# Two-block transformer kernel: where the last two modulation slabs of each layer are multiplied, and on which token tile the layer's output product begins

## The reference, cut to what matters

```python
def ada_params(sc, w, b):          # sc (n, 1024), w (1024, 6144)
    mod = sc @ w + b
    return [t[:, None, :] for t in jnp.split(mod, 6, axis=-1)]

def conv_glu(x, w_in, conv_w, conv_b, w_out):      # first block, both layers
    gate, val = jnp.split(x @ w_in, 2, axis=-1)    # 2 x 2816 columns
    gate = lax.conv_general_dilated(gate, conv_w[:, None, :], ...) + conv_b
    return (jax.nn.gelu(gate, approximate=False) * val) @ w_out

# first block, each layer:
x = layer_norm(ALPHA * x + h, ...)                       # after the mixer
x = layer_norm(ALPHA * x + memory_cross_attention(...), ...)
x = layer_norm(ALPHA * x + conv_glu(x, ...), ...)
# second block: ada_params(silu(c), ada_w[i], ada_b[i]) for its layers i = 0, 1
```

## Time and profile before

| | |
|---|---|
| median of 3 runs | 2130.54 us (2127.76 to 2132.85) |
| the profiled execution, its own time | 2126.64 us |
| its span in the trace | 2124.9 us |
| busy: PE / DVE / ACT / POOL | 1931.2 / 1083.8 / 994.5 / 1258.8 us |
| read from DRAM | 339.65 MB, 160 GB/s over the span |
| mean granted PE clock | 0.963 |

### The profile page before, as it was taken

The page is one execution under the profiler, slowest core; times in us unless marked ns, Lnnn a source line. Parts: engine busy times, 40 slices in busy tenths (PEclk is TensorE's granted clock), DMA queues, the critical chain, the costliest instruction groups (busy, mean ns, idle before and its releaser), DMA issues.

```text
span 2124.9 us, 33890 instructions
## 1 busy us (share of the span) xinstructions
PE 1931.2 (91%) x13581; PEld 1704.6 (80%) x13581; DVE 1083.8 (51%) x1511; ACT 994.5 (47%) x1718; POOL 1258.8 (59%) x588
## 2 busy tenths in 40 slices
PE   6879989999899979989999889998879998978997
PEld 6868888877899966868877868876669987948996
DVE  7783146641100073136657655678767942846641
ACT  3453435443444373434554444478744546425542
POOL 9647566678688602646669334300468885426995
PEclk9999999999899999999999999999989998989999
DMA  6325367764555503357774212211235553314552
GB/s 251 139 93 186 112 224 293 302 259 175 177 181 190 187 1 139 119 220 279 298 274 161 80 62 97 99 60 64 86 135 182 181 194 121 119 61 164 182 192 104
DMA packets 48321, 342.30 MB, mean 161 GB/s; under 512 B 5264, under 2 KB 6288, under 8 KB 7248
## 3 DMA queue, kind: packets, MB, share of 16 engines
q1 hardware_dynamic: 45968, 328.22, 42.3%
q0 software_dynamic: 2240, 12.49, 1.5%
HBM read 339.65 MB, written 1.05 MB: 160 GB/s over the span
## 4 chain that ended last, share of the span: by engine, by line
PE 65%; DVE 17%; ACT 7%; POOL 5%; issue 5%; DMA 1%; DVEq 0%; POOLq 0%; SPq 0%; ACTq 0%
PE bank L1664 11%; PE bank L1668 11%; PE bank L1666 11%; PE bank L1718 11%; DVE arena L902 2%; POOL w_lo L2146 2%; PE bank L1762 2%; PE bank L1277 2%; POOL w_hi L2146 2%; PE bank L1279 2%; PE bank L1280 2%; PE bank L1699 2%; PE bank L1698 2%; PE bank L1696 2%; ACT arena L1102 2%
## 5 line engine op out<-in xcount | busy, mean ns | idle before, releaser
L2146 POOL TENSOR_TENSOR w_lo<-ring,w_hi 128x1024 fp32r<-128x1024 f32 x360 | 876.8, 2461 | 314.4 <-ACT w_hi L2696 313.9
L1664 PE MATMUL bank<-x_hi,w_hi 128*128 128x256 f32 x2176 | 615.7, 283 | 29.9 <-POOL w_lo L2146 16.6
L1668 PE MATMUL bank<-x_lo,w_hi 128*128 128x256 f32 x2176 | 618.4, 284 | 0.0
L2696 ACT ACTIVATE w_hi<-ring 128x1024 fp32r<-128x1024 f32 x448 | 448.7, 1052 | 348.8 <-DMA ring<-slabs_dram 344.7
L1664 PEld LDWEIGHTS bank<-x_hi,w_hi 128*128 128x128 f32 x2176 | 414.4, 190 | 50.5 <-issue 50.5
L1668 PEld LDWEIGHTS bank<-x_lo,w_hi 128*128 128x128 f32 x2176 | 413.6, 190 | 0.0
L1666 PE MATMUL bank<-x_hi,w_lo 128*128 128x256 f32 x1472 | 413.4, 281 | 0.0
L1666 PEld LDWEIGHTS bank<-x_hi,w_lo 128*128 128x128 f32 x1472 | 281.3, 191 | 0.0
L2146 POOL TENSOR_TENSOR w_hi<-ring,w_hi 128x1024 fp32r<-128x1024 f32 x88 | 208.8, 2394 | 110.9 <-ACT w_hi L2696 110.9
L2634 ACT ACTIVATE arena<-bank 128x512 f32<-128x512 f32 (+1 forms) x182 | 100.1, 563 | 296.9 <-PE bank L1668 190.8
L1666 PE MATMUL bank<-x_hi,w_hi 128*128 128x256 f32 x704 | 197.5, 281 | 0.0
(11 more groups left out here) (341 smaller groups left out, 3657.9 us busy)
## 6 DMA issues: line engine op xcount, KB each, us to landing
ring<-slabs_dram SPq DMA_DIRECT2D x312, 1024.0 KB, 4.8
lnrow<-ln_dram POOLq DMA_DIRECT2D x6, 1024.0 KB, 5.0
xt<-xT_dram SPq DMA_DIRECT2D x1, 1024.0 KB, 5.9
xt<-memT_dram POOLq DMA_DIRECT2D x1, 1024.0 KB, 14.0
x<-x_dram POOLq DMA_DIRECT2D x1, 1024.0 KB, 17.9
arena<-ctx_dram POOLq DMA_DIRECT2D x1, 1024.0 KB, 7.0
lnrow<-ln_dram POOLq DMA_DIRECT2D x2, 512.0 KB, 4.8
res<-x POOLq DMA_DIRECT2D x2, 512.0 KB, 3.2
```

What stands on the lines that cost most here:

```text
L1664: ins = pe.matmul(dst, wh[:, k, c], src[0][:, k, :], start=(k == 0), stop=False)
L1668: ins = pe.matmul(dst, wh[:, k, c], src[1][:, k, :], start=False, stop=(k == KC - 1))
L2146: pool.tensor_tensor(dst[:, c], ring[:, s, c], w_hi[:, s, c].bitcast(F32), ALU.subtract).then_inc(S["lo_ready"], 1)
L2696: a.activation(w_hi[:, g % RING, c], ring[:, g % RING, c], ACT.Copy) \
```

## The change

The four modulation slabs 22 and 23 of both layers leave the stream: `f0` and `f1` have 44 slabs, the ring sees 308 loads. The four are loaded into two places of their own in the arena (`aside`), two after output slab 4 of `fo0`, two after slab 2 of `xq1` (the second cross attention's query weights). PE multiplies them in the norm that follows (`late_ada`): the first before the transposes of the first token tile, the second between the two tiles. For layer 0 that is the norm after `fo0`, for layer 1 the norm ahead of network 1. ACT copies them out (`late_out`), DVE turns them (`turn_late`), ACT keeps the columns (`late_columns`). Layer 0's last four chunks are added to the bias with layer 1's.

`rows_split` of `fo0` and `fo1` waits for banks 2 and 3 only, runs slab 0 on the second token tile, waits for banks 0 and 1, and runs slab 0 on the first. ACT makes `hi` of output slab 0 one chunk earlier and of slab 1 where slab 0's was. `ctx` and `wdt` are loaded after POOL's last `lo` of `f1`.

```diff
+ASIDE = {"f0": 2, "f1": 2}
-    STAGES.append((_name, _n))
+    STAGES.append((_name, _n - ASIDE.get(_name, 0)))
...
+        aside = [cut(11264, KC, 256), cut(16384, KC, 256)]
+        late_raw = xT[:, 5:7, :]
+        late_turn = [xT[:, 7, :], xT[:, 0, :]]
...
             def rows_split(stage, src=(h_hi, h_lo), n_slabs=FC // 2, ready=("hT_ready", 2), hook=None):
-                for b_ in (0, 1, 2, 3):
+                second_first = stage in ("fo0", "fo1")
+                for b_ in (2, 3) if second_first else (0, 1, 2, 3):
                     pe.wait_ge(free_of(b_), frees(b_))
...
                     ready_for(j)
+                    if j == 0 and second_first:
+                        tile(j, 1, (0, 1), (0, 1), True)
+                        for b_ in (0, 1):
+                            pe.wait_ge(free_of(b_), frees(b_))
+                        tile(j, 0, (0, 1), (0, 1), False)
+                        continue
...
+            def late_ada(layer, e):
+                b = 6 + e
+                pe.wait_ge(aside_landed[e], 16 * (layer + 1))
+                pe.wait_ge(free_of(b), frees(b))
+                for k in range(KC):
+                    q = 32 * (k % 4)
+                    ins = pe.matmul(bank[b][q:q + 32, 0:256], sc_in[:, k, :], aside[e][:, k, :],
+                                    start=(k < 4), stop=(k >= 4))
+                fill(ins, b, "act")
...
-                    col_T_split(stage, 2 * u + 41, u)
-                ada(stage, 4, 2, 10)
-                ada(stage, 5, 3, 10, last_one=True)
+                    col_T_split(stage, 2 * u + 41, u, last_net=u == 1)
...
-            tokens_to_T(by_class=True)
+            late_ada(0, 0)
+            tokens_to_T(by_class=True, between=lambda: late_ada(0, 1))
...
-            tokens_to_T(used_up=True)
+            late_ada(1, 0)
+            tokens_to_T(used_up=True, between=lambda: late_ada(1, 1))
...
                 if k in (1, 4):
                     los(f"f{k // 4}", 1, 2)
+                    if k == 4:
+                        pool.dma_start(ctxN[:, :, :], ctx_in).then_inc(S["in_ctx"], 16)
+                        pool.dma_start(wdt[:, :, :], wdt_in).then_inc(S["in_wdt"], 16)
...
+                for layer, at in enumerate((FIRST["fo0"] + 4, FIRST["xq1"] + 2)):
+                    if g == at:
+                        for e in range(2):
+                            sp.dma_start(aside[e].rearrange("p a b -> p (a b)"),
+                                         slabs[AT[f"f{layer}"] + 44 + e]) \
+                                .then_inc(aside_landed[e], 16)
...
+            def turn_late(layer):
+                for e in range(2):
+                    v.wait_ge(free["act"][6 + e], marks["late"][layer][6 + e])
+                    v.transpose(late_turn[e], late_raw[:, e, :]).then_inc(S["late_turned"], 1)
+                    v.wait_ge(S["late_turned"], L.own("late_turned"))
...
-                        elif n == FC - 1:
-                            hi(out_, 0)
+                        else:
+                            hi(out_, n + 2 - FC)
```

More of the change, by code:

```diff
@@ L89 @@
     _at += _n
-SLABS = _at
-assert SLABS % RING == 0
+STREAM = _at
+SLABS = sum(_n for _name, _n in DRAM)
+assert STREAM % RING == 0
 RUNS = [("dq", "dwo"), ("xq0", "xk1"), ("gq0", "gwo"), ("xq1", "f1")]
@@ L188, in build @@
         landed = [ctx.enter_context(nc.semaphore(f"slab_landed{s}")) for s in range(RING)]
+        aside_landed = [ctx.enter_context(nc.semaphore(f"aside_landed{s}")) for s in range(2)]
         full = {r: [ctx.enter_context(nc.semaphore(f"full_{r}{b}")) for b in range(8)]
@@ L1886, in ada @@
                                     start=(k < 4), stop=(k >= 4))
-                    begun(ins, k == 0 and last_one)
                 fill(ins, b, "dve")
+            def late_ada(layer, e):
[7 more added lines that the diff above has]
+                fill(ins, b, "act")
+                marks.setdefault("late", {}).setdefault(layer, {})[b] = L.now(("act", b))
             def ada_columns(layer):
                 pe.wait_ge(free_of(4), frees(4))
-                pe.wait_ge(S["ada_kept"], 24 * (layer + 1))
+                pe.wait_ge(S["ada_kept"], 22 * (layer + 1))
+                if layer:
+                    pe.wait_ge(S["late_kept"], 4)
+                n = (22, 24)[layer]
                 kept = modC.rearrange("p u (c q s) -> p q (u c) s", c=2, q=4)
+                late = late_cols.rearrange("p u (c q s) -> p q (u c) s", c=2, q=4)
                 for q in range(4):
-                    ins = pe.matmul(bank[4][32 * q:32 * (q + 1), 0:96].rearrange("p (a s) -> p a s", s=2),
-                                    pick, kept[:, q, :, :], start=True, stop=True)
+                    part = bank[4][32 * q:32 * (q + 1), :].rearrange("p (a s) -> p a s", s=2)
+                    ins = pe.matmul(part[:, 0:2 * n, :], pick, kept[:, q, 0:2 * n, :],
+                                    start=True, stop=True)
+                    if layer:
+                        ins = pe.matmul(part[:, 48:52, :], pick, late[:, q, :, :],
+                                        start=True, stop=True)
                 fill(ins, 4, "dve")
@@ L2230, in _ @@
             for layer in range(2):
-                for n in range(2, FC):
-                    halves_read[FIRST[f"f{layer}"] + 2 * n + 1] = marks[f"lo_f{layer}"] + 2 * (n - 1)
-            for g in range(SLABS):
+                for n in range(FC):
+                    halves_read[FIRST[f"f{layer}"] + 2 * n + 1 + RING] = marks[f"lo_f{layer}"] + 2 * (n + 1)
+            for g in range(STREAM):
                 if g in halves_read:
@@ L2653, in proj_N, with late_out, late_columns, x_to_T @@
                              bank[u][:, :].rearrange("p (t c) -> p t c", t=NT))
-            def x_to_T(by_class=False):
+            def late_out(e):
+                copy_out(6 + e, late_raw[:, e, :], bank[6 + e][:, 0:256])
+            def late_columns(dst):
+                for e in range(2):
+                    a.wait_ge(S["late_turned"], L.took("late_turned"))
+                    a.activation(dst[:, e, :].rearrange("p (c s) -> p c s", s=2),
+                                 late_turn[e].rearrange("p (c s) -> p c s", s=32)[:, :, 0:2],
+                                 ACT.Copy).then_inc(S["late_kept"], 1)
+            def x_to_T(by_class=False, late=False):
                 for tt in range(NT):
@@ L2659, in x_to_T @@
                         b, ck = 4 + 2 * tt + q, slice(4 * q, 4 * q + 4)
+                        if late and q == 0:
+                            late_out(tt)
                         a.wait_ge(full["act"][b], L.filled(b))
@@ L2871, in _ @@
             hi("gq0", 1)
[L2872 removed]
+            x_to_T(by_class=True, late=True)
             a.wait_ge(S["qscale_ready"], DIL_HEADS)
```

54 lines of the change are left out of this document (30 added, 24 removed).

## The result

The changed kernel takes 2113.42 us (median of 5 runs, 2110.81 to 2114.51). The kernel before, beside it, took 2130.54 us (2123.14 to 2132.85). The ratio is 0.9929, with an interval of 0.9917 to 0.9941. The prediction was 2115.4 us, so 15.1 us less; 17.1 came. Run once more with other runs of the kernel before, the changed kernel took 2113.99 us, ratio 0.9922 (0.9909 to 0.9936), 14.6 us less. So the forecast size lies between the two measurements. (In the rounds of the experiments, with 11 to 29 runs each, the median of the kernel before was 2128.2 to 2129.1 us, so 17.1 is on the high side.)

What follows compares the result with a forecast made beforehand. PE, busy 91% of the span, was taken as the bound, so only its standing still or running slowly mattered. 6.95 + 6.98 + 1.6 - 0.4 = 15.1 us off 2130.54 gave 2115.4 us, range 2108 to 2123.

Steps and rivals of the forecast that it cites:

- 1. The ends of both networks: At `fo0` and `fo1`, slab 0 is ready early and slab 1 starts 6.95 and 6.98 us sooner.
- 2. The products in the gaps: In the norms, modulation products moved into PE's gaps before the transposes fit there and cost nothing.
- 3. DVE's turns: Ahead of network 1, DVE's two turns stand before `x_lo` and cost 0.95 us, bounds 0.5 and 1.2.
- 4. Network 1's start: Moving `ctx` and `wdt` removes PE's 2.51 us stall at 958.89; less 0.95 for DVE's turns, net gain 1.6 us.
- the difference, 2.5 us, is the stall: At network 1's start, slab load of 9.8 against 7.3 us beside `ctx`: this 2.5 us was taken as PE's stall.
- The price of `ctx` at its new place: Beside output slabs 2 and 3, the moved load delays them 3.4 us if taken in full; the sum counted nothing.
- 5 and 6: 5: loads aside in `fo0` and `xq1` cost 0, bound 2.4 us each. 6: middle of `fo1` loses 0.4 us.
- Slab 0 was not late: Rival at both network ends: slab 0 is still late, half of part 1 lost, gain 8, 2122.5 us; chance 0.12.
- the stream did not suffer: Rival: loads aside delay a slab at both places and the 958.89 stall stays, gain 7.8, 2122.7 us; chance 0.10.
- the lower clock did not last longer behind the gaps: Rival in both norms: late products as short bursts prolong the low clock; 25 us more in each gives 2140 us; chance 0.03.
- More comes back by the clock: Rival: late products shorten low-clock stretches after 534 and at 940.11, up to 2.5 and 1.7 us; gain 19, 2111.5 us; chance 0.12.

Runs made afterwards that it cites:

- the two experiments on the old stream: Kernel before with one edit each: output slab 0 on the second token tile first, ratio 1.0009; `ctx` and `wdt` loaded after POOL's last subtraction, ratio 1.0008.
- one edit: Kernel before, with only slab 0 of both output products on the second token tile first, waiting for banks 2 and 3 only: 2128.35 us, ratio 1.0009.

## Why the prediction was right

**1. The ends of both networks.** Forecast 6.95 and 6.98, measured 6.8 and 7.0. From the last network matmul to slab 1 of `fo1` it took 13.24 us before (the modulation products, the wait and slab 0) and takes 6.22 now; in `fo0` 13.21 and 6.45. (The table's 7.1 and 6.3 have all of network 0 in them.) Every step of the working is in the profile: ACT takes slab 0 after chunk 20's product and does not wait for the load, POOL is done 0.75 us ahead of PE (0.9 worked out), the wait for banks 0 and 1 is 0.25 to 0.35 (0.1), slab 1 follows at once. Two things make the number: the idle time, and that the clock no longer falls behind it.

**2. The products in the gaps** take no time of PE's path themselves, doubled too. But network 1 starts 1.15 us more slowly in every kernel that has them (below), and the prediction put this part at nothing. That the products are the cause is not shown.

**3. DVE's turns** cost 0.96 us at the wait, as worked out (0.95); 0.5 to 0.7 of it come back when they stand behind `x_lo`.

**4. Network 1's start: the right number for a wrong reason.** Forecast was that the stall of 2.51 us goes, and that `ctx` was its cause. The stall went, and with it the smaller ones behind it, 3.0 us in all. But alone the move took 1.5 us from the stall, lost 0.8 two pairs on and 2.2 at `fo1`; and undone in the changed kernel it costs 0.4 at most. The step that failed is "the difference, 2.5 us, is the stall". The load did become faster, by 1.5 us alone and by 2.0 in the changed kernel, but the step took for granted that all of this stands on PE's path and that the network would start as before. That 1.6 us net came out near what was measured here (3.0 less 1.0 for the turns) is luck. The Trainium skill, DMA: Bandwidth & Descriptors, section Issuing engines are not separate DMA queues, says that transfers started by different engines interleave on the same 16 engines. The trace agrees: the pair's second slab landed in 9.8 and 8.9 us beside `ctx` and in 6.9 us without it. The price of `ctx` at its new place was put at 3.4 us if taken in full: in the kernel before it cost 2.2, in the changed kernel nothing, since there the slabs beside it are two ahead of PE. So the zero in the sum was right, because of which slabs these were.

**5 and 6.** The loads aside delay nothing that can be seen. Slab 3 of `fo1` waited 1.38 us, 0.2 more than before (0.4 forecast), and that stall was worth removing in itself. The other 0.5 us of the last row of the table lie behind slab 3, and the two experiments on the old stream have them too.

**The rivals.** Slab 0 was not late, the stream did not suffer, and the lower clock did not last longer behind the gaps. "More comes back by the clock" looked right in the first profile (2.1 us from `gq0` to `gwo`) and was scatter. Against it, network 1 now starts slower: the windows at its start, in the changed kernel,

```profile
936.00:940.00 4.00, 4.00 (x26) 2.74 (x27) 0.67 (x2) 0.26 (x1) 4.00 (x2) 0.50 0.29 98
940.00:944.00 4.00, 4.00 (x29) 4.00 (x29) 0.00 (x0) 0.00 (x0) 0.09 (x1) 0.77 0.98 410
```

show the lower level from 936 to some 2 us behind 940, 5.9 us behind the first product. Before, it ended 3.3 us behind it. The second modulation product thus came 9.5 us behind the first one, not 8.3. The 3.0 us that the body gained are net of this 1.15. The lower level is no longer than it was, but it comes later in the norm. The windows that it fills, before and then after:

```profile
933.20:943.30 10.10, 5.42 (x30) 3.37 (x31) 7.25 (x12) 3.08 (x4) 5.33 (x6) 0.50 0.49 187
```

```profile
931.60:941.80 10.20, 6.97 (x38) 5.31 (x39) 4.86 (x8) 3.22 (x6) 5.28 (x3) 0.50 0.49 177
```

Before, it began 2.8 us ahead of the second tile's transposes (935.96), in PE's idle stretch. Now it begins 0.7 us behind them (930.84), and its end falls on the network's first chunk. This repeats: the second modulation product comes 9.35 to 9.66 us behind the first in all ten profiles with the change's stream, and 8.34 to 8.47 in the three without. The turns are not the cause (9.66 with them behind `x_lo`), nor is the product between the tiles by itself (9.57 with both in front). No run leaves the late products out of this norm, so whether they are is open.

## What to carry to other kernels

Where two engines' results gate the same instruction, find the second release before forecasting the gain of removing the first; here one edit was worth nothing alone, and 5 us more beside the other. Work that is removed from under a stall only lengthens the stall; it pays when the slots it frees let the late input start earlier. And before a stretch of one profile is called an effect, profile the same kernel twice: here code that nobody touched moved by 2 to 5 us.

## What was not expected of the hardware

The same idle stretch in the same code is followed by the lower clock in one execution and not in another: the 24 matmuls above show it, behind 1.90 and 1.89 us. The largest difference lies ahead of network 0, in code that all the kernels share. The windows of the changed kernel and then of the kernel before:

```profile
290.00:296.50 6.50, 5.78 (x27) 5.78 (x28) 0.00 (x0) 0.35 (x1) 5.32 (x3) 0.50 0.41 161
```

```profile
290.00:296.50 6.50, 6.50 (x58) 6.50 (x57) 0.00 (x0) 1.84 (x2) 4.86 (x3) 1.00 0.45 161
```

PE had stood 3.49 us in the one (until 290.72) and 3.21 us in the other (until 289.50). Behind it 6.5 us ran at 0.50 in the one and at 1.00 in the other, 27 matmuls against 58. It is not just that the one stood longer: with DVE's turns behind `x_lo` PE stood 3.52 us there, and the clock stayed at 1.00. But length counts: the four profiles with 3.26 us or less kept 1.00, and the seven with 3.76 us or more all ran a part of what followed at 0.50. The 6.5 us at half the clock are most of the 3.9 us by which the changed kernel's profile reached network 0 later, and why the spans of two profiles differed by 13.4 us where the medians differed by 17.1. In the thirteen profiled executions of this case network 0's first product came anywhere from 300.7 to 306.3 us, by and large the later the more time PE had spent at the lower level ahead of it (17 us at 300.7, 31 us at 306.3, but also some 20 us at 303.9).
